# Layer norms of a two-block network on one core: statistics by column groups of the array, and a product of low rank in place of mean and shift

## The chip, the core and the metric

The kernel runs on one core of a Trainium2 chip. Its engines are TensorE (PE; its weight loads are listed as PEld), VectorE (DVE), ScalarE (ACT), GpSimd (POOL) and SyncE (SP), which issues most transfers. The metric is the device time of one execution in microseconds; less is better.

## The reference

Two blocks follow each other, in float32, on 512 tokens of 1024 features. The first has a gated delta net and a dilated attention, each with a SwiGLU feed-forward. The second is of concern here: two layers on the latents x (512 tokens, stream s=0) and on a context (256 tokens, s=1). Each layer is as follows, with ALPHA = sqrt(2) and D = 1024:

```
def layer_norm(x):
    mu = jnp.mean(xf, -1, keepdims=True)
    var = jnp.mean(jnp.square(xf - mu), -1, keepdims=True)
    return ((xf - mu) * lax.rsqrt(var + LN_EPS)).astype(x.dtype)

def modulate(x, shift, scale):
    return layer_norm(x) * (1 + scale) + shift
...
    h, hc = modulate(x, sh1, sc1), modulate(ctx, sh1x, sc1x)
    y, yc = mixing_sublayer(h, hc, ...)
    x = layer_norm(ALPHA * x + g1 * y) * ln1_g[l] + ln1_b[l]
    x = layer_norm(ALPHA * x + g2 * swiglu(modulate(x, sh2, sc2), w_ffn_in[l], w_ffn_out[l])) * ln2_g[l] + ln2_b[l]
```

The context goes the same way, but is dropped after the mixing of the second layer. So a norm is often followed at once by a second one with a modulation: normalise, scale and shift, normalise again, modulate.

## The kernel before

Everything lies transposed: a tile is 128 features (partitions) by 512 tokens of the latents or 256 of the context, and there are eight tiles, k = 0 to 7, to 1024 features. The sums of a norm go over partitions and over tiles, so TensorE makes them. Each engine has its own instruction stream, written out by hand in functions whose names begin with the engine (pe_, dve_, act_, pool_); `at(...)` and `done(...)` name semaphore values, so the order on an engine is the order of the calls.

A weight product is split: activations and weights have a high part (fp32r) and a low part, and each tile is three matmuls (high by high, low by high, high by low). `pe_products` does the mixing's products (lines L484 to L486), `pe_ffn_in` the FFN's gate and up products (L720 to L722), `pe_ffn_out` its down products (L743 to L745). The FFN works in eleven chunks; beside chunk c of the gate and up products stand the down products of chunk c-1. The products that come first after a norm are called the head here: for each tile k three pieces of the mixing (nine matmuls), or twelve matmuls of the FFN, so that they can begin when tile 0 is there.

There are five norms of the latents and three of the context in the second block: N_IN (before a mixing; in layer 1 with the end of layer 0's second norm ahead of it), N_POST (after a mixing) and N_END. The steps of one:

- `pe_stat(N, s, k)`, when tile k of the sum and its square are there. The activations are the weights of the array, 128x128 a time, and the moving side has two to four columns, ones or products of the gain (L915, and L922 for the squares); L919 adds constants. These stand between the products of the last chunk that make the tiles.
- `dve_rows` and `act_rows`: means, variances and inverse deviations, tokens on partitions, in columns of 4 or 2.
- `pe_spread`: spreads a column over all partitions, 128 tokens a matmul (L1010), and `act_spread` copies one of two to SBUF.
- for each tile, `dve_scale` (times the inverse deviation, from PSUM, L1038), `pool_centre` (less mean, L1047), `act_affine` (scale and shift); for a double norm once more; then `act_norm_part` makes the high part and `dve_norm_part` the low part (L1067), which the product of the tile waits for.

`pe_read`, the splits of weights (L566 and L665 on VectorE, L389 on ScalarE, a helper's line for all its work) and the gating of the FFN (GpSimd's casts, `pool ... R<-U`) go on beside this. The kernel sets PSUM banks by a rotating list; `PS.keep` holds one until `PS.release`.

Of the kernel before, what the change touches and what calls it, by code (L numbers as in the profile page):

```python
# [27 lines left out]
K_ID, K_ONE, K_BONE, K_EPS, K_SEL, K_RES = 0, 128, 256, 384, 389, 392  # L28
# [9 lines left out]
def constants():  # L38
# [9 lines left out]
    for s in range(2):  # L48
        k[s::32, K_SEL + s] = 1
    g = K_GDN  # L50
# [216 lines left out]
class Norm:  # L267
# [3 lines left out]
    def __init__(self, tag, streams, ready, first, to=None, second=None, key=None, h=None, hi=None, lo=None):  # L271
        self.tag, self.streams, self.ready, self.first, self.to = tag, streams, ready, first, to
        self.second, self.key, self.h, self.hi, self.lo = second, key, h, hi, lo


def build(nc, a, out):
    ctx = ExitStack()
    with ctx:
# [32 lines left out]
        by_vector = KC[:, K_SEL:K_SEL + 2]  # L311
        e1, e64, ea2, one1, e128 = (KC[:, K_EPS + n:K_EPS + n + 1] for n in range(5))
# [178 lines left out]
        def pe_products(pieces, wh, lead=1, between={}):  # L491
# [6 lines left out]
            for what, p, n, s in steps(pieces, lead):  # L498
# [21 lines left out]
                for g in group:  # L520
                    if s == (last if early else g.ends_on()):
                        pe_read(g)
                if (s, p.n) in between and early:
                    between[s, p.n]()
# [166 lines left out]
        def pe_ffn(tag, ns, then=None, mid={}, between={}, last=None):  # L691
            for c in range(12):
                if c in mid:
                    mid[c]()
                if c < 11:
                    pe_ffn_in(tag, ns, c, between)
                if c:
                    pe_ffn_out(tag, ns, c - 1, then, last)

        def pe_ffn_in(tag, ns, c, between):  # L700
# [6 lines left out]
            for i, group in enumerate(groups):  # L707
                if c == 0 and i in between:
                    between[i]()
                for j, s, p in group:  # L710
                    bank("ffn", tag, c, j, s, p)
                    pe.wait_ge(*at("wi lo", tag, c, p))
                for k in range(8):
                    for j, s, p in group:
# [8 lines left out]
                        if k == 7:  # L723
                            t.then_inc(*pe.done("product", "ffn", tag, c, j, s, p))
            pe.mark("gate up", tag, c)
            if c == 0 and "end" in between:
                between["end"]()
# [61 lines left out]
        def act_ffn(tag, ns, then=None, early=None, mid={}, taken=()):  # L789

            for c in range(12):
# [8 lines left out]
                if c < 10:  # L800
                    act_ffn_w_in(tag, c + 1)
                if c < 11:
# [10 lines left out]
        def dve_ffn(tag, ns, take_out, then=None, early=None, mid={}, taken=(), last=None):  # L813
            for c in range(12):
# [12 lines left out]
                if c == 10:  # L827
                    dve_ffn_w_out(tag, c)
                if c == 11 and early:
# [39 lines left out]
        def dve_ffn1(tag, before, l, then=None, early=None, mid={}, last=None):  # L869
# [12 lines left out]
        WZ = view(U[:, NB:NB + 48], (8, 6))  # L882
        AGB = U[:, NB + 48:NB + 64]
        CS = U[:, NB + 64:NB + 72]
        ROW = [view(U[:, NB + 72:NB + 168], (24, 4)), view(U[:, NB + 168:NB + 216], (24, 2))]
        (R_S, R_SG, R_SGG, R_SGB, R_Q, R_QGG, R_M, R_MM, R_V, R_R, R_MR, R_A, R_E, R_F, R_M2, R_W, R_V2, R_R2, R_MR2,
         R_T, R_R2A) = range(21)

        def pool_norm_weights(N, o):

            g, b = COL[:, o:o + 8], COL[:, o + 8:o + 16]
            pool.e.memset(WZ[:, :, 0], 1.0).then_inc(*pool.done("norm weights", N.tag, 0))
            pool.e.tensor_copy(WZ[:, :, 1], g).then_inc(*pool.done("norm weights", N.tag, 1))
            pool.e.tensor_tensor(WZ[:, :, 2], g, g, M).then_inc(*pool.done("norm weights", N.tag, 2))
# [2435 lines left out]
```

## Time and profile before

| | |
|---|---|
| three runs | 3733.38, 3730.15, 3723.03 us; median 3730.15 |
| the profiled execution | 3729.26 us, of it the span 3727.5 us |
| TensorE busy | 3461.7 us, 93% |
| VectorE, ScalarE, GpSimd busy | 1593.8, 1215.1, 283.6 us |
| granted TensorE clock, mean | 0.945 of full |

The profile is of one execution. The fp32 matmuls on this chip show as two records each in it, the fp32r ones as one. Lines such as L915 are those of the kernel's file. A granted clock of 1.00 is the 2.4 GHz level, 0.50 the 1.2 GHz level; a number between them is a stretch with both.

### The profile page before, as it was taken

What the parts mean: (1) busy time and instruction counts of PE and PEld (TensorE: products, weight loads), DVE (VectorE), ACT (ScalarE), POOL (GpSimd) and SP (SyncE); (2) the same over time, 40 slices, a digit from 0 to 9 for tenths busy, and PEclk for the clock granted to TensorE, in tenths of its full rate; (3) what the DMA queues carried; (4) which work ended last, traced back from release to release, by engine and by line L of the source; (5) the groups of instructions that cost most, each with busy time, mean ns of one, the idle gap of its engine ahead of it and who ended that gap; (6) DMA issues with size and microseconds to landing.
All of it is one profiled execution on the core that took longest, in us unless ns stands there. A gap on an engine that the chain in (4) does not pass through costs nothing.

```text
span 3727.5 us, 42969 instructions
## 1 busy us (share of the span) xinstructions
PE 3461.7 (93%) x18282; PEld 2891.3 (78%) x18282; DVE 1593.8 (43%) x2811; ACT 1215.1 (33%) x2006; POOL 283.6 (8%) x368
## 2 busy tenths in 40 slices
PE   7798989999999889999979978999999889889998
PEld 5685967887778768888766777888888777678887
DVE  4645544444323444344225545334443425543443
ACT  6547232212434322123224535111111425441112
POOL 1101000000000000011000003000000301020001
PEclk9899999999999899999988989999997899989998
DMA  3101021132226223131125211111110112011310
GB/s 128 41 23 68 1 91 68 68 136 79 71 90 241 71 86 113 68 113 55 46 74 200 91 46 68 68 68 68 68 44 20 38 46 94 1 68 68 136 68 34
DMA packets 190543, 282.00 MB, mean 76 GB/s; under 512 B 18952, under 2 KB 121864, under 8 KB 190224
## 3 DMA queue, kind: packets, MB, share of 16 engines
q1 hardware_dynamic: 188176, 272.19, 20.7%
q10 hardware_dynamic: 2176, 7.08, 0.6%
q8 instruction: 143, 2.34, 0.3%
q14 instruction: 48, 0.39, 0.0%
HBM read 274.00 MB, written 2.10 MB: 74 GB/s over the span
## 4 chain that ended last, share of the span: by engine, by line
PE 85%; ACT 6%; DVE 5%; POOL 2%; issue 1%; DMA 1%; SPq 1%; ACTq 0%; POOLq 0%; DVEq 0%
PE ps L720 9%; PE ps L721 9%; PE ps L722 9%; PE ps L743 5%; PE ps L484 5%; PE ps L745 5%; PE ps L744 5%; PE ps L485 5%; PE ps L486 5%; PE ps L380 3%; PE ps L374 3%; PE ps L1129 3%; ACT U L389 2%; PE ps L546 2%; PE ps L547 2%; PE ps L548 2%
## 5 line engine op out<-in xcount | busy, mean ns | idle before, releaser
L389 ACT ACTIVATE R<-ring 128x1024 fp32r<-128x1024 f32 (+4 forms) x285 | 396.6, 1415 | 1068.5 <-PE ps L722 539.6
L720 PE MATMUL ps<-R,R 128*128 128x512 f32 (+1 forms) x1760 | 657.6, 374 | 43.9 <-DVE R L665 21.2
L721 PE MATMUL ps<-R,R 128*128 128x512 f32 (+1 forms) x1760 | 654.7, 372 | 0.0
L722 PE MATMUL ps<-R,R 128*128 128x512 f32 (+1 forms) x1760 | 654.1, 372 | 0.0
L484 PE MATMUL ps<-R,R 128*128 128x512 f32 (+1 forms) x1016 | 421.8, 415 | 60.7 <-DVE ringlo L566 26.3
L720 PEld LDWEIGHTS ps<-R,R 128*128 128x128 f32 x1760 | 336.7, 191 | 106.1 <-DVE R L665 22.9
L485 PE MATMUL ps<-R,R 128*128 128x512 f32 (+1 forms) x1016 | 392.5, 386 | 0.0
L486 PE MATMUL ps<-R,ringlo 128*128 128x512 f32 (+1 forms) x1016 | 391.0, 385 | 0.0
L722 PEld LDWEIGHTS ps<-R,R 128*128 128x128 f32 x1760 | 336.0, 191 | 56.9
L721 PEld LDWEIGHTS ps<-R,R 128*128 128x128 f32 x1760 | 336.7, 191 | 56.0
L665 DVE TENSOR_TENSOR R<-ring,R 128x2048 fp32r<-128x2048 f32 x88 | 197.9, 2288 | 355.4 <-ACT R L389 355.4
L566 DVE TENSOR_TENSOR ringlo<-ring,R 128x1024 fp32r<-128x1024 f32 (+3 forms) x153 | 175.2, 1155 | 384.5 <-ACT R L389 384.5
L743 PE MATMUL ps<-R,R 128*128 128x512 f32 (+1 forms) x880 | 334.3, 380 | 3.1 <-DVE U L945 3.1
L745 PE MATMUL ps<-R,R 128*128 128x512 f32 (+1 forms) x880 | 329.5, 374 | 0.0
L744 PE MATMUL ps<-R,R 128*128 128x512 f32 (+1 forms) x880 | 329.5, 374 | 0.0
L389 ACT ACTIVATE U<-ps 128x512 f32<-128x512 f32 (+3 forms) x324 | 174.1, 553 | 440.5 <-PE ps L380 284.8
L484 PEld LDWEIGHTS ps<-R,R 128*128 128x128 f32 x1016 | 201.3, 198 | 119.3 <-DVE ringlo L566 25.9
L774 DVE TENSOR_TENSOR U<-SQ,ps 128x512 f32<-128x512 f32 (+1 forms) x110 | 69.5, 632 | 465.8 <-PE ps L722 302.5
L485 PEld LDWEIGHTS ps<-R,R 128*128 128x128 f32 x1016 | 201.5, 198 | 45.6 <-issue 12.7
L486 PEld LDWEIGHTS ps<-R,ringlo 128*128 128x128 f32 x1016 | 200.6, 197 | 37.9
L380 PE MATMUL ps<-KC,U 128*128 128x128 f32 (+2 forms) x1028 | 159.8, 295 | 50.6 <-DVE U L1853 15.6
L389 ACT ACTIVATE SQ<-ps 128x512 f32<-128x512 f32 (+1 forms) x147 | 80.5, 547 | 379.0 <-PE ps L722 375.0
(238 smaller groups left out, 4944.2 us busy)
## 6 DMA issues: line engine op xcount, KB each, us to landing
ring<-in_w_mod SPq DMA_DIRECT2D x24, 2048.0 KB, 9.4
ring<-in_ffn_w_in SPq DMA_DIRECT2D x44, 1024.0 KB, 10.9
ring<-in_w_ffn_in SPq DMA_DIRECT2D x44, 1024.0 KB, 11.3
ring<-in_ffn_w_out SPq DMA_DIRECT2D x10, 2048.0 KB, 7.7
ring<-in_w_ffn_out SPq DMA_DIRECT2D x10, 2048.0 KB, 7.8
ring<-in_dil_w_in SPq DMA_DIRECT2D x9, 2048.0 KB, 7.7
ring<-in_gdn_w_in SPq DMA_DIRECT2D x8, 2048.0 KB, 8.7
ring<-in_w_o SPq DMA_DIRECT2D x6, 2048.0 KB, 8.2
```

The costliest lines, as they stand in the source:

```text
L380: x = pe.e.transpose(o, i, ident[0:k, 0:k])
L389: return act.e.activation(o, i, fn, **kw)
L484: pe.e.matmul(ps[:, 0:x.n], hi[:, k, :], x.hi[k], start=(k == 0), stop=False)
L485: pe.e.matmul(ps[:, 0:x.n], hi[:, k, :], x.lo[k], start=False, stop=False)
L486: return pe.e.matmul(ps[:, 0:x.n], lo[:, k, :], x.hi[k], start=False, stop=(k == p.kt - 1))
L665: dve.e.tensor_tensor(WI[p][1], ffn_in_half(tag, c, p, ring), WI[p][0], SUB).then_inc(*dve.done("wi lo", tag, c, p))
L720: pe.e.matmul(ps, w[0], x[0], start=(k == 0), stop=False)
L721: pe.e.matmul(ps, w[0], x[1], start=False, stop=False)
L722: t = pe.e.matmul(ps, w[1], x[0], start=False, stop=(k == 7))
L743: pe.e.matmul(ps[:, 0:n], w[0], x[0], start=(k == 0), stop=False)
L744: pe.e.matmul(ps[:, 0:n], w[0], x[1], start=False, stop=False)
L745: t = pe.e.matmul(ps[:, 0:n], w[1], x[0], start=False, stop=(k == 1))
```

## The change

The norm is computed in another form. With r the inverse deviation and m the mean of a token, gain a and shift b of a feature, LN(x)*a + b is x*a*r plus a sum of a few products of a column (over features) by a row (over tokens): J = 2 terms for a single norm, 4 for a double one, whose two stages become one.

- **Statistics.** `pe_stat(N, P, s, p)` takes a pair of tiles p. The weights are 32 columns wide (`P.wz`), the activations and their squares move, 512 or 256 columns, and the four matmuls go to four column groups of the array (`tile_position=(0, 32 * g)`). `act_sums` copies the result to SBUF and `pe_sums` adds the groups with small matmuls of six columns, which also turns tokens onto partitions.
- **Weights of the norm.** `pool_norm_weights` (some 30 tiny operations), `dve_norm_weights`, `pe_norm_columns` (transposes), `act_norm_columns` and `dve_norm_consts` make columns and constants ahead of time, in a place `P` of SBUF. In FFN2 of layer 0 GpSimd's wait for the gate and up products of chunk 10 and stand ahead of the last chunk's casts.
- **Spread and rows.** `pe_spread` spreads one column and transposes the rows' high and low parts. `pe_rank(N, P, s, k)` is one fp32r product of 3J = 12 or 6 rows by 512 or 256 columns.
- **Tile.** `dve_scale` (x times gain column times spread row), `dve_add` (plus the rank product from PSUM), then high and low part as before. GpSimd's centring and ScalarE's affine operations are gone from here.
- **Residual.** What the double norm keeps for the residual, ALPHA*y, is made later: `pe_residual`, `act_residual`, `pool_residual` (two GpSimd operations a tile), `act_y`. In FFN2 it runs in chunk 1, in the second mixing layer behind the head.
- **Heads.** `pe_products` goes over the head's pieces tile by tile for both streams now, and calls `between[s](k)` after tile k; `pe_ffn_in` calls "tile" likewise. These issue the rank product of tile k+2.

```diff
                 early = lead > 1 and p in head
-                group = [p] if not early or s != last else head if p is head[-1] else []
+                group = [p] if not early else head if p is head[-1] else []
                 for g in group:
                     bank(*product_name(g, g.n, s))
+                    if early:
+                        PS.keep(*product_name(g, g.n, s))
                     pe.wait_ge(*at("w lo", g.tag, g.n))
                 for k in range(p.kt):
                     for g in group:
                         t = pe_tile(g, s, PS.of(*product_name(g, g.n, s)), k)
                         if k == p.kt - 1:
                             t.then_inc(*pe.done(*product_name(g, g.n, s)))
+                    if early and group and s in between:
+                        between[s](k)
...
+                    if c == 0 and s == 0 and "tile" in between:
+                        between["tile"](k)
...
-        def pe_stat(N, s, k, square=None):
...
-            for b in range(n // 128):
-                pe.e.matmul(ps[:, 8 * b:8 * b + w1.shape[1]], XS[s][:, k, b * 128:(b + 1) * 128], w1,
-                            start=(k == 0 and b == 0), stop=False)
-            if consts:
-                for j in range(8):
-                    pe.e.matmul(ps[:, 32:37], ones, WZ[:, j, 1:6], start=False, stop=False)
-            pe.wait_ge(*at("square", N.tag, s, k))
-            for b in range(n // 128):
-                t = pe.e.matmul(ps[:, 8 * b + 4:8 * b + 6], q[:, b * 128:(b + 1) * 128], w2, start=False,
-                                stop=(last and b == n // 128 - 1))
...
+            for k in (2 * p, 2 * p + 1):
+                pe.wait_ge(*at(*N.ready(s, k)))
+                pe.wait_ge(*at("square", N.tag, s, k))
+            for g, k in enumerate((2 * p, 2 * p + 1) * 2):
+                q = SQ.of(N.tag, s, k) if square is None else square[:, k, :]
+                t = pe.e.matmul(ps[32 * g:32 * g + 32, 0:n], P.wz[:, k, :], XS[s][:, k, :] if g < 2 else q[:, 0:n],
+                                start=(p == 0), stop=(p == 3), tile_position=(0, 32 * g))
+                if g > 1:
+                    t.then_inc(*pe.done("sq read", N.tag, s, k))
...
+            activate(rr[:, 0:n], PS.of("stat", N.tag, s)[:, 0:n], ACT.Copy).then_inc(*act.done("ps", "stat", N.tag, s))
...
+                t = pe.e.matmul(ps[:, 8 * b:8 * b + 6], RR.of("sums", N.tag, s)[:, b * 128:(b + 1) * 128], by_sum,
+                                start=True, stop=True)
...
+        def pe_spread(N, s):
+
+            n, J = NS2[s], N.J
+            ps = bank("spread", N.tag, s)
+            PS.keep("spread", N.tag, s)
+            pe.wait_ge(*at("rows", N.tag, s))
+            spread(ps, s, R_R if N.gain is None else R_RR, ("spread", N.tag, s))
+            ps = bank("rows", N.tag, s)
+            pe.wait_ge(*at("row parts", N.tag, s))
+            tp([(ps[0:3 * J, b * 128:(b + 1) * 128], RWF[s][:, b, 0:3 * J]) for b in range(n // 128)]).then_inc(
+                *pe.done("rows turned", N.tag, s))
...
+            pe.e.matmul(ps[:, 0:n], P.ct[s][0:3 * J, k * 128:(k + 1) * 128], P.rt[s][0:3 * J, 0:n], start=True,
+                        stop=True).then_inc(*pe.done("rank", N.tag, s, k))
...
+            dve.e.scalar_tensor_tensor(norm_to(N, s)[:, k, :], XS[s][:, k, :], AK[s][:, k:k + 1],
+                                       PS.of("spread", N.tag, s)[:, 0:NS2[s]], M, M).then_inc(
...
+            dve.wait_ge(*at("rank", N.tag, s, k))
+            dve.e.tensor_tensor(h, h, PS.of("rank", N.tag, s, k)[:, 0:NS2[s]], A_).then_inc(
...
+        def dve_tile(N, s, i):
+
+            if i < 8:
+                dve_scale(N, s, i)
+                dve_add(N, s, i)
+            if N.hi and i:
+                dve_norm_part(N, s, i - 1)
...
+            pool.e.tensor_tensor(x, x, r, M).then_inc(*pool.done("y scaled", N.tag, s, k))
...
+            pool.e.tensor_tensor(x, x, mr, SUB).then_inc(*pool.done("y centred", N.tag, s, k))
...
-            dve.e.tensor_tensor(dst[:, k, :], src[:, k, :], spread_of(N, s, part)[0], M).then_inc(
...
-            pool.e.tensor_tensor(dst[:, k, :], dst[:, k, :], RR.of("spread", N.tag, s, part)[:, 0:NS2[s]], SUB).then_inc(
...
-            activate(dst[:, k, :], dst[:, k, :], ACT.Identity, scale=g(s, k), bias=b(s, k)).then_inc(
...
+            def tile(k):
+                if k < 6:
+                    pe_rank(N, P_O, 0, k + 2)
+                if k == 7:
+                    PS.release("spread", N.tag, 0)
+                    pe_residual(N, 0)
...
-            act_ffn(tag, ns, taken=[(0, 1), (1, 1)])
+
+            def y():
+                for k in range(8):
+                    act_y(N, 0, k)
+
+            def columns_():
+                act_norm_columns(N_IN[1] if l == 0 else N_END, P_FFN)
+            act_ffn(tag, ns, mid={1: lambda: act_residual(N, 0), **({8: columns_} if l else {11: columns_})},
+                    taken=[(0, 1), (1, 1)], inner={1: y})
```

The orders of instructions show three places. The names in them: R tiles hold high and low parts, U and X activations, KC constants, ps PSUM.

TensorE in the last chunk of layer 0's first FFN of the second block, down products of the latents, before:

```order
L743 MATMUL ps<-R_1024_66,R_2048_60 128x512
L744 MATMUL ps<-R_1024_67,R_2048_60 128x512
L745 MATMUL ps<-R_1024_66,R_2048_61 128x512
L743 MATMUL ps<-R_1024_66,R_2048_60 128x512
L744 MATMUL ps<-R_1024_67,R_2048_60 128x512
L745 MATMUL ps<-R_1024_66,R_2048_61 128x512
L915 MATMUL ps<-U,X 128x4 x4
L922 MATMUL ps<-U,SQ 128x2 [waits act_result]
L922 MATMUL ps<-U,SQ 128x2 x3
L1010 MATMUL ps<-KC,U 128x128 [waits dve_result]
L1010 MATMUL ps<-KC,U 128x128 x3
```

and after:

```order
L767 MATMUL ps<-R_1024_66,R_2048_60 128x512
L768 MATMUL ps<-R_1024_67,R_2048_60 128x512
L769 MATMUL ps<-R_1024_66,R_2048_61 128x512
L1028 MATMUL ps<-X,U 32x512 [waits dve_result,act_result]
L1028 MATMUL ps<-X,U 32x512
L1028 MATMUL ps<-SQ,U 32x512 x2
L1130 MATMUL ps<-KC,U 128x128 [waits dve_result]
L1130 MATMUL ps<-KC,U 128x128
L393 MATMUL ps<-KC,U 12x128 [waits dve_result]
L393 MATMUL ps<-KC,U 12x128
```

Behind two products of one tile stood eight narrow matmuls for the statistics of one tile; now four wide ones for a pair of tiles stand behind the products. The context's spread stays where it was (L1010, now L1130) and two transposes (L393) follow it.

TensorE in the head of FFN2, layer 0, where tile 0 ends and tile 1 begins, before:

```order
L722 MATMUL ps<-R_4096_56,R_2048_61 128x512
L720 MATMUL ps<-R_4096_56,R_2048_62 128x512
L721 MATMUL ps<-R_4096_57,R_2048_62 128x512
L722 MATMUL ps<-R_4096_56,R_2048_63 128x512
L720 MATMUL ps<-R_4096_56,R_2048_60 128x512 [waits dve_result]
L721 MATMUL ps<-R_4096_57,R_2048_60 128x512
L722 MATMUL ps<-R_4096_56,R_2048_61 128x512
```

and after:

```order
L741 MATMUL ps<-R_4096_56,R_2048_62 128x512
L742 MATMUL ps<-R_4096_57,R_2048_62 128x512
L743 MATMUL ps<-R_4096_56,R_2048_63 128x512
L1160 MATMUL ps<-R_512_72,R_1024_69 128x512 [waits dve_result]
L741 MATMUL ps<-R_4096_56,R_2048_60 128x512 [waits dve_result]
L742 MATMUL ps<-R_4096_57,R_2048_60 128x512
L743 MATMUL ps<-R_4096_56,R_2048_61 128x512
```

A rank product (L1160), that of tile 2, has come in between the twelve matmuls of tile 0 and those of tile 1, which wait for VectorE in both.

VectorE in the head of FFN2, layer 1, one round and more, before:

```order
L1038 TENSOR_TENSOR X<-X,ps 128x512
L1038 TENSOR_TENSOR U<-X,ps 128x512 [waits act_result]
L1067 TENSOR_TENSOR R_4096_57<-U,R_4096_56 128x512 [waits act_result]
L1038 TENSOR_TENSOR X<-X,ps 128x512
L1038 TENSOR_TENSOR U<-X,ps 128x512 [waits act_result]
L1067 TENSOR_TENSOR R_4096_57<-U,R_4096_56 128x512 [waits act_result]
```

and after:

```order
L1170 SCALAR_TENSOR_TENSOR U<-X,U,ps 128x512
L1180 TENSOR_TENSOR U<-U,ps 128x512 [waits pe_result,dve_result]
L1190 TENSOR_TENSOR R_4096_57<-U,R_4096_56 128x512 [waits act_result]
L1170 SCALAR_TENSOR_TENSOR U<-X,U,ps 128x512
L1180 TENSOR_TENSOR U<-U,ps 128x512 [waits pe_result,dve_result]
L1190 TENSOR_TENSOR R_4096_57<-U,R_4096_56 128x512 [waits act_result]
```

The second L1038 (the double norm's second scale) is gone; the add L1180 waits for the rank product and stands ahead of the low part of the tile before (L1190).

## Rows read from the trace of the kernel before

**Rows 1.** The page, parts 1 and 4: busy time by engine; the chain that ended last.
```profile
PE 3461.7 (93%) x18282; PEld 2891.3 (78%) x18282; DVE 1593.8 (43%) x2811; ACT 1215.1 (33%) x2006; POOL 283.6 (8%) x368
...
PE 85%; ACT 6%; DVE 5%; POOL 2%; issue 1%; DMA 1%; SPq 1%; ACTq 0%; POOLq 0%; DVEq 0%
```

**Rows 2.** Windows over the span, PE alone, of L915, L922, L919, L1010 in turn.
```profile
0.00:3727.50 3727.50, 63.41 (x416) 0.95 0.22 76
...
0.00:3727.50 3727.50, 68.78 (x416) 0.95 0.22 76
...
0.00:3727.50 3727.50, 5.78 (x48) 0.95 0.22 76
...
0.00:3727.50 3727.50, 29.46 (x168) 0.95 0.22 76
```

**Rows 3.** Windows: length, busy us (instructions) by engine, PEclk, DMA share, GB/s.
```profile
2831.00:2857.00 26.00, 26.00 (x127) 24.84 (x125) 7.18 (x11) 5.70 (x11) 0.00 (x0) 0.56 0.00 1
2857.00:2907.00 50.00, 46.87 (x184) 43.30 (x184) 12.87 (x42) 12.87 (x25) 5.14 (x7) 0.50 0.00 1
3080.00:3090.00 10.00, 5.69 (x37) 4.50 (x35) 0.85 (x3) 2.05 (x4) 3.42 (x3) 1.00 0.46 157
3706.00:3728.00 22.00, 4.42 (x19) 4.03 (x19) 5.88 (x14) 8.88 (x12) 9.83 (x8) 0.50 0.25 95
```

**Rows 4.** Timeline of PE, first product of a mixing head, then of its next piece; likewise FFN.
```profile
1736.96 0.50 PE L484 MATMUL ps<-R,R 128*128 128x512 f32 x1 [2.27 <-DVE R L1067]
...
1756.12 0.77 PE L484 MATMUL ps<-R,R 128*128 128x512 f32 x1 [2.56 <-DVE ringlo L566]
...
2295.42 0.77 PE L720 MATMUL ps<-R,R 128*128 128x512 f32 x1 [5.63 <-ACT SQ L389]
...
2326.95 0.79 PE L720 MATMUL ps<-R,R 128*128 128x512 f32 x1 [5.28 <-DVE R L665]
```

**Rows 5.** Timeline of PE: start, us, operation, count; a product in four column groups.
```profile
1156.89 1.92 PE L1251 MATMUL ps<-ring,SCT 128*32 128x512 f32 x16 [0.69 <-ACT U L389]
1158.74 0.49 PE L1985 MATMUL ps<-U 64*128 64x128 f32 x4
```

**Rows 6.** Groups by shape, PE: transposes of 128 columns.
```profile
L380 PE MATMUL ps<-KC,U 128*128 128x128 f32 x992 | 154.5, 297 | 42.4 <-DVE U L1853 15.6 <-DVE U L2818 12.7 <-ACT U L389 7.5
```

**Rows 7.** Timeline of PE: products at either level of the clock, and spreads.
```profile
2299.59 0.39 PE L720 MATMUL ps<-R,R 128*128 128x512 f32 x1
2299.82 0.40 PE L721 MATMUL ps<-R,R 128*128 128x512 f32 x1
...
2868.30 0.63 PE L743 MATMUL ps<-R,R 128*128 128x512 f32 x1
2868.73 0.63 PE L744 MATMUL ps<-R,R 128*128 128x512 f32 x1
...
2921.42 1.95 PE L1010 MATMUL ps<-KC,U 128*128 128x128 f32 x16
```

**Rows 8.** Groups by shape, VectorE and GpSimd: count, busy us, mean ns, idle before.
```profile
L3080 DVE SCALAR_TENSOR_TENSOR X<-ps,MOD,X 128x512 f32<-128x512 f32 x176 | 119.6, 744 | 34.2 <-PE ps L745 34.1
...
L1067 DVE TENSOR_TENSOR R<-U,R 128x512 fp32r<-128x512 f32 x32 | 37.0, 1156 | 26.7 <-ACT R L389 26.7
...
L1038 DVE TENSOR_TENSOR U<-X,ps 128x512 f32<-128x512 f32 x32 | 21.6, 679 | 9.2 <-ACT X L389 7.8 <-PE ps L1010 1.3
...
L1047 POOL TENSOR_TENSOR X<-X,RR 128x512 f32<-128x512 f32 x32 | 40.6, 1283 | 133.7 <-ACT RR L389 119.4 <-DVE X L1038 14.3
```

**Rows 9.** Timeline of DVE, the low part in a mixing and in an FFN head.
```profile
1742.51 0.70 DVE L1067 TENSOR_TENSOR R<-U,R 128x512 fp32r<-128x512 f32 x1 [0.40 <-ACT R L389]
...
2308.48 1.50 DVE L1067 TENSOR_TENSOR R<-U,R 128x512 fp32r<-128x512 f32 x1 [1.51 <-ACT R L389]
```

**Rows 10.** Timeline of all engines, the end of the span.
```profile
3706.67 0.18 DVE L945 COPY U<-ps 128x24 f32<-128x24 f32 x1 [5.42 <-PE ps L922]
...
3714.32 9.83 POOL L1047 TENSOR_TENSOR X<-X,RR 128x512 f32<-128x512 f32 x8 [43.23 <-ACT RR L389]
```

More of the change, by code:

```diff
@@ L49, in constants @@
         k[s::32, K_SEL + s] = 1
+    for n in range(4):
+        k[n, K_SUM + n] = k[32 + n, K_SUM + n] = 1
+    for n in (64, 96):
+        k[n, K_SUM + 4] = k[n + 2, K_SUM + 5] = 1
     g = K_GDN
@@ L696, in pe_ffn @@
                     pe_ffn_in(tag, ns, c, between)
+                if c == 11 and "last" in between:
+                    between["last"]()
                 if c:
@@ L811, in act_ffn, with dve_ffn @@
                     act_square(X[:, k, :], S, then, k)
-        def dve_ffn(tag, ns, take_out, then=None, early=None, mid={}, taken=(), last=None):
+        def dve_ffn(tag, ns, take_out, then=None, early=None, mid={}, taken=(), last=None, inner={}):
             for c in range(12):
@@ new lines, in dve_norm_weights @@
+        def dve_norm_weights(N, P):
+            J = N.J
+            if N.gain is not None:
+                dve.wait_ge(*at("norm sums", N.tag))
+                dve.e.reduce_sum(P.g5s, P.g5, AX).then_inc(*dve.done("norm sum", N.tag))
+            dve.wait_ge(*at("norm weights", N.tag))
+            for s in N.streams:
+                dve.e.tensor_tensor(P.cbr[s][:, :, 2 * J:3 * J], P.cb[s][:, :, 0:J], P.cbr[s][:, :, 0:J], SUB).then_inc(
+                    *dve.done("norm column", N.tag, s))
@@ new lines, in pe_norm_columns @@
+        def pe_norm_columns(N, P):
+            for s in N.streams:
+                for i in range(2):
+                    ps = bank("columns", N.tag, s, i)
+                    pe.wait_ge(*at("norm column", N.tag, s))
+                    tp([(ps[0:3 * N.J, k * 128:(k + 1) * 128], P.cbf[s][:, 4 * i + k, 0:3 * N.J]) for k in range(4)]
+                       ).then_inc(*pe.done("columns", N.tag, s, i))
+            if N.gain is not None:
+                ps = bank("consts", N.tag)
+                pe.wait_ge(*at("norm sum", N.tag))
+                pe.e.matmul(ps[:, 0:5], ones, P.g5s, start=True, stop=True).then_inc(*pe.done("consts", N.tag))
@@ L1043, in pool_centre, with spread @@
-        def pool_centre(N, s, k, part):
-            dst = N.h[s] if part else N.to[s] if N.to else XS[s]
-            pool.wait_ge(*at("scaled", N.tag, s, part, k))
-            pool.wait_ge(*at("spread mean", N.tag, s, part))
-            pool.e.tensor_tensor(dst[:, k, :], dst[:, k, :], RR.of("spread", N.tag, s, part)[:, 0:NS2[s]], SUB).then_inc(
-                *pool.done("centred", N.tag, s, part, k))
-            if k == 7:
-                pool.mark("rr read", "spread", N.tag, s, part)
-        def act_affine(N, s, k, part):
-            dst = N.h[s] if part else N.to[s] if N.to else XS[s]
-            g, b = (N.second if part else N.first)
-            act.wait_ge(*at("centred", N.tag, s, part, k))
-            activate(dst[:, k, :], dst[:, k, :], ACT.Identity, scale=g(s, k), bias=b(s, k)).then_inc(
-                *act.done("h" if part else "y", N.tag, s, k))
+        def spread(o, s, row, name):
+            for b in range(NS2[s] // 128):
+                t = pe.e.matmul(o[:, b * 128:(b + 1) * 128], ROW[s][:, row, b:b + 1].broadcast_to([128, 128]), ident,
+                                start=True, stop=True)
+            t.then_inc(*pe.done(*name))
@@ L2535, in pe_in, with context @@
-            pe_products(in_pieces(l), WHM[l], 3, between)
+            N, P = N_IN[l], P_FFN
+            def context(k):
+                if l and k < 6:
+                    pe_rank(N, P, 1, k + 2)
+                if l == 0 and k == 0:
+                    pe_stat(N, P, 0, 3)
+                if l == 0 and k == 1:
+                    pe_sums(N, 0)
+                if l and k == 7:
+                    PS.release("spread", N.tag, 1)
+                if k == 6 - 2 * l:
+                    pe_spread(N, 0)
+                if k == 7:
+                    pe_rank(N, P, 0, 0)
+                    pe_rank(N, P, 0, 1)
```

737 lines of the change are left out of this document (423 added, 314 removed).

## The prediction

> **What bounds the kernel now.** I read the page first: TensorE is busy for 93% of the span and makes 85% of the chain that ended last [rows 1]. So what comes off TensorE counts in full, unless TensorE then waits for another engine. Next I read the changed lines over the whole span [rows 2]: the statistics (L915, L922, L919) hold TensorE for 63.41 + 68.78 + 5.78 = 138.0 us in 880 records, the spreads (L1010) for 29.46 us in 168. A record takes 5.78/48 = 0.12 us for the constants, at the full clock, and 132.2/832 = 0.16 in the mean of the others, for two to five moving columns. Then I read the granted clock by stretch [rows 3]: from 2831 to 2907 us, where the statistics stand between down products of the second block's first FFN, it is 0.56 and then 0.50, although TensorE is busy for 46.87 of the last 50 us. Last I read the heads of the products that follow a norm [rows 4, 9]: there TensorE runs products nearly back to back, and VectorE makes the tiles just ahead of it.
>
> The sum is made against the profiled execution, 3729.26 us (span 3727.5), 0.9 us under the median of the three runs, 3730.15. A measurement of this kernel can tell about 0.3%, 11 us, from no change.
>
> **Statistics, -104.** Each pair of tiles of the latents now takes four fp32 matmuls of 512 columns in four column groups; each pair of the context four of 256. The nearest row is another fp32 product in four column groups, L1251 [rows 5]: its 16 records start at 1156.89 and the next line starts at 1158.74, 1.85 us. With two records a matmul that is eight matmuls, two rounds of four groups, if the groups run side by side; a pair is one round, 0.93 us. I take 1.0, and 0.57 for the context. There are 20 and 12 pairs: 26.8 us. The 26 small matmuls of the sums are 52 records; 16 spread records took 1.95 us [rows 7], 0.12 each: 6.3 us. With 1 us for three constant matmuls that is 34, for 138: -104. If the groups ran one after another, a pair would cost up to four times as much, 4 x 0.93 and 4 x 0.43: (3.7 - 1.0) x 20 + (1.7 - 0.57) x 12 = +68. Against it: the row's 16 records would then take 0.12 us each, while even an fp32r product of 512 columns starts its next only after 0.23 [rows 7].
>
> How the array is entered is a place where notes and rows can be weighed. The row shows nothing between L1251 and its neighbour beyond the 1.85 us, so the sum has only the rounding up from 0.93 to 1.0. The Trainium skill ("TensorEngine Tiling (Array Packing)", Key Properties) says that changing the tiling mode drains TensorE. An estimate for such a drain is what a product lasts beyond the next start, 0.39 - 0.23 = 0.16 us [rows 7]; with a change in and out of 32 groups that would be 10 us, where the sum has some 4.
>
> **Spreads, transposes, ranks, +10.** 29.5 us go. What comes: 54 fp32 spreads, 108 records of 0.12, 13 us; 90 transposes, priced by 992 of 128 columns in 154.5 us [rows 6], 0.155 each, 14 us; 40 fp32r rank products of 512 columns at 0.23 [rows 7] and 24 of 256 at half of it, 12 us.
>
> **Clock, -16.** Products of 512 columns start every 0.43 us at the half level and every 0.23 at the full one [rows 7]. From 2831 to 2907 stand 48 such at the half level, and 30 of 256 columns. As the near-empty matmuls around them go, I take them at the full level: 48 x 0.20 + 30 x 0.09 = 12, and 4 more in small stretches elsewhere. The bound on the other side is nothing, if the stretch keeps its level.
>
> **The rank loop, +47.** In a head the program issues rank k+2 on TensorE after product k, while VectorE works in the order scale i, add i (waits for rank i), low part i-1. Product k+1 waits for low part k+1; that stands behind add k+2, which waits for rank k+2, which stands behind product k. So TensorE can't run on; its order is product k, rank k+2, idle for the add and the low part, product k+1. Only the scale lies under the product. Prices: the add as L1038, 0.68 us [rows 8], the low part 0.70 where nothing disturbs it [rows 9], the rank until its end 0.39 [rows 7], some 0.05 for hand-overs. In a mixing head a step is nine matmuls, 2.05 us; a period becomes 3.85. Before, the head takes from 1736.96 to 1756.12 less the last wait of 2.56 [rows 4], 16.6 us; afterwards seven periods and a product, 29: +12. In an FFN head a step is twelve matmuls, 2.74 us; a period becomes 4.54, the head 34.5 us. Before, it takes from 2295.42 to 2326.95 less 5.28 [rows 4], 26.3 us: there the start is at the half clock and VectorE and GpSimd pace it. +8. Two heads of each kind make +40. The context's head of the second mixing layer, 256 columns, has a period of some 2.24 by the same sum, 16.8 us for about 10 now: +7. Behind the heads TensorE waits for a weight split, 5.28 us [rows 4]; VectorE gets no free time for it in the longer head, so nothing is given back. If a step's waits were all hidden the term would be nothing; a low part as slow as its mean, 1.16 [rows 8], would make it +62.
>
> Here a rule bears. The rows show the low part at 1.50 us in an FFN head, where GpSimd's L1047 runs, and at 0.70 in a mixing head [rows 9]; I let it be 0.70 afterwards, since GpSimd's work leaves the heads. The Trainium skill ("SBUF — State Buffer", Two separate sides) says that VectorE and GpSimd share a pair of ports and that the loser is blocked for the whole operation; the trace agrees.
>
> **The residual elsewhere, +12.** The 64 GpSimd operations of 1.28 us [rows 8] no longer pace the heads, but in each FFN2 sixteen of them, 20.5 us, stand ahead of chunk 1's casts, which its down products wait for, and eight affine operations stand ahead of ScalarE's silu. A chunk of these products lasts about as long as the head, 25 us or more, so most is covered; what sticks out I take as 3 us in each layer. The tiny operations of the norm's weights wait on GpSimd for the gate and up products of the last chunk and stand ahead of its casts: +3. In the second mixing layer the residual's copies and spreads stand ahead of the next weight split: +3. With the covers gone each would be some 10; fully covered, nothing.
>
> **The tail, 0.** Before, the last norm runs from 3706.67 to the end, GpSimd's eight centrings being 9.83 us of it [rows 10]. Afterwards VectorE does a scale with a column, 0.744, and an add, 0.68, per tile [rows 8], 11.4 us; no affine follows the last, but a copy, the sums' matmuls and a transpose stand ahead. These even out to within 2 us.
>
> Sum: -104 + 10 - 16 + 47 + 12 = -51, 3729.3 - 51 = **3678 us**.
>
> **The rivals.**
> (a) The loop costs nothing, because tiles are ready early. For it: the heads run nearly back to back now. Against: the order leaves no rank in stock behind the first two. Then 3678 - 47 = 3631.
> (b) The other side, slower. In the loop TensorE is busy for 2.05 of 3.85 us or 2.74 of 4.54, and the granted clock may fall to the half level in it. Twelve products then cost 12 x 0.20 = 2.4 us more and the rank 0.2: two FFN heads of eight steps +42, two mixing heads (nine products, 2.0) +32, the context's +7: +81, to 3759. It decides from 63 us of these on, some three quarters of the steps. For it: after long idle the clock was low, 0.50 from 3706 on. Against: from 3080 to 3090 TensorE was busy for only 5.69 of 10 us in short pieces, and the clock was 1.00 [rows 3].
> (c) The clock of 2831 to 2907 isn't won back and the covers of the residual fail in part: +16 and some +17: 3711.
> (d) The column groups run one after another: 3678 + 68 = 3746. The row of L1251 speaks against it.
>
> **How the numbers follow.** The forecast has 0.58, its own range 3655 to 3700 (the clock's 16 and the loop's size either way); (a) 0.13, (c) 0.14, (b) 0.11, (d) 0.04. The range from 3635 to 3738 leaves out (b), (d) and a part of (a). Faster, under 3719: the forecast, (a) and half of (c), 0.79; within 0.3%: the rest of (c) and edges of (b), 0.08; slower: most of (b) and (d), 0.13.
>
> **What would show it.** Afterwards: the statistics of a pair in some 1 us, four groups starting together; TensorE waiting for VectorE's low part in each of the eight steps of a head, 1.4 to 1.8 us each; heads longer by 8 to 12 us; the clock near 1.0 from 2800 on to the next idle; GpSimd busy in FFN2's second chunk instead of the heads; a span near 3676. Wrong if the heads show no wait in each step (a), if their matmuls start every 0.43 us (b), if the four groups start one after another (d), or if chunk 1 shows a new wait of over 5 us on casts (c).

## The result and the profile after

The change made the kernel slower: 3772.51 us median of four runs, against 3726.59 before in the same series, a ratio of 1.0127 (95% interval 1.0098 to 1.0156), 46 us. Forecast were 3678 us, in 3635 to 3738.

The page of the changed kernel, parts 1 and 4:

```profile
span 3772.1 us, 42206 instructions
## 1 busy us (share of the span) xinstructions
PE 3444.7 (91%) x17810; PEld 2808.0 (74%) x17810; DVE 1609.8 (43%) x2884; ACT 1175.3 (31%) x1960; POOL 263.5 (7%) x410
...
PE 84%; DVE 6%; ACT 6%; issue 1%; DMA 1%; POOL 1%; ACTq 0%; SPq 0%; DVEq 0%; POOLq 0%
```

TensorE is busy for 17 us less, not for over 100 less [rows 1], and the span is longer by 44.6 us. The rest of the span is idle time of TensorE: 327 us now, 266 before.

What the statistics cost on TensorE is as forecast. Here is a pair of tiles of the latents on TensorE's timeline with the products beside it (two lines each for the activations and the squares, two records a line):

```profile
2278.07 0.39 PE L499 MATMUL ps<-R,ringlo 128*128 128x512 f32 x1
2278.39 0.62 PE L1028 MATMUL ps<-X,U 128*32 128x512 f32 x2
2278.41 0.62 PE L1028 MATMUL ps<-SQ,U 128*32 128x512 f32 x2
2278.85 0.60 PE L1028 MATMUL ps<-X,U 128*32 128x512 f32 x2
2278.86 0.60 PE L1028 MATMUL ps<-SQ,U 128*32 128x512 f32 x2
2279.39 0.50 PE L497 MATMUL ps<-R,R 128*128 128x512 f32 x1
```

All four column groups start within 0.02 us; from 2278.39 to the next product at 2279.39 it is 1.00 us, as I had taken, and 0.09 more ahead of it, since a further product would have followed the L499 of 2278.07 after 0.23. The groups by shape of the new lines (the two lines of L1028 lie over each other, so their 22.8 us are one and the same time):

```profile
L1028 PE MATMUL ps<-SQ,U 128*32 128x512 f32 x80 | 22.8, 650 | 0.0
...
L1028 PE MATMUL ps<-X,U 128*32 128x512 f32 x80 | 22.8, 647 | 11.8 <-ACT SQ L402 11.8
...
L1130 PE MATMUL ps<-KC,U 128*128 128x128 f32 x108 | 18.2, 324 | 18.2 <-DVE U L1114 14.4 <-DVE U L1099 3.1 <-DVE U L1170 0.7
...
L1160 PE MATMUL ps<-R,R 12*128 12x512 f32 x24 | 12.5, 541 | 0.7 <-ACT R L402 0.7
...
L1049 PE MATMUL ps<-KC,RR 128*128 128x6 f32 x52 | 7.6, 267 | 5.5 <-ACT RR L402 5.5
```

TensorE's waits, with total, times and longest:

```profile
PE ps L497 <- DVE R L1190: 25.4, 18, 2.7
...
PE ps L741 <- DVE R L1190: 20.0, 13, 2.6
...
PE ps L1130 <- DVE U L1114: 14.4, 4, 4.9
...
PE ps L1028 <- ACT SQ L402: 13.4, 8, 4.8
...
PE ps L1049 <- ACT RR L402: 5.5, 5, 3.0
```

The wait for the low part (L1190) is 45.4 us in 31 places; before it was 14.8 us for L1067 in 11. The waits of L1028 and L1049 are new, and the spreads (L1130) wait 18.2 us for rows, as the row of their group says, against 11.3 before.

The first mixing head on TensorE, three of its steps:

```profile
1743.03 0.51 PE L497 MATMUL ps<-R,R 128*128 128x512 f32 x1 [1.45 <-DVE R L1190]
...
1747.24 0.50 PE L497 MATMUL ps<-R,R 128*128 128x512 f32 x1 [1.45 <-DVE R L1190]
...
1750.47 0.79 PE L1160 MATMUL ps<-R,R 6*128 6x512 f32 x1
1752.72 0.79 PE L497 MATMUL ps<-R,R 128*128 128x512 f32 x1 [1.45 <-DVE R L1190]
1753.31 0.63 PE L498 MATMUL ps<-R,R 128*128 128x512 f32 x1
1753.73 0.63 PE L499 MATMUL ps<-R,ringlo 128*128 128x512 f32 x1
...
1756.85 0.79 PE L1160 MATMUL ps<-R,R 6*128 6x512 f32 x1
1759.49 0.80 PE L497 MATMUL ps<-R,R 128*128 128x512 f32 x1 [1.85 <-DVE R L1190]
```

From 1743.03 to 1747.24 a step takes 4.21 us: the nine products at the full clock, the rank product, 1.45 us idle. From 1752.72 to 1759.49 it takes 6.77 us, and the products (L498 at 1753.31, L499 at 1753.73) start every 0.42 us. VectorE in the step that ends at 1747.24:

```profile
1742.89 0.74 DVE L1170 SCALAR_TENSOR_TENSOR U<-X,U,ps 128x512 f32<-128x512 f32 x1
1745.90 0.69 DVE L1180 TENSOR_TENSOR U<-U,ps 128x512 f32<-128x512 f32 x1 [2.27 <-PE ps L1160]
1746.50 0.68 DVE L1190 TENSOR_TENSOR R<-U,R 128x512 fp32r<-128x512 f32 x1
```

The scale is done early; the add waits 2.27 us for the rank product, and the low part stands behind it. That is the loop that the prediction drew. The windows tell what it had not drawn in: the first mixing head, the first FFN head, the two stretches of [rows 3], and one in an attention.

```profile
1725.00:1767.00 42.00, 32.16 (x78) 21.15 (x78) 12.92 (x20) 4.32 (x8) 4.94 (x8) 0.64 0.10 33
2307.00:2353.00 46.00, 37.08 (x111) 26.58 (x112) 14.52 (x23) 6.28 (x9) 1.01 (x2) 0.76 0.00 0
2831.00:2857.00 26.00, 26.00 (x142) 22.64 (x141) 8.06 (x13) 2.90 (x3) 7.66 (x32) 1.00 0.19 61
2857.00:2907.00 50.00, 38.35 (x238) 26.38 (x236) 25.62 (x69) 16.82 (x33) 0.00 (x0) 0.88 0.00 1
2038.00:2076.00 38.00, 38.00 (x139) 24.66 (x137) 15.05 (x50) 16.53 (x54) 0.00 (x0) 0.51 0.18 63
```

The granted clock is 0.64 and 0.76 in the heads. From 2831 to 2857 it is 1.00, where it had been 0.56 [rows 3], and from 2857 to 2907 it is 0.88 in place of 0.50.

Where the 44.6 us of the two spans lie I read by laying the n-th matmul of a product's line in one trace beside the n-th in the other (columns: stretch in the trace before, how much later the changed kernel is at its end than at its beginning):

| stretch before, us | change, us |
|---|---|
| up to 1480 | +3.0 |
| statistics and rows of the norms: 1480 to 1737, 2191 to 2295, 2791 to 2916, 3250 to 3321, 3638 to the end | -81 |
| head of the first mixing, 1737 to 1756 | +24.6 |
| FFN head of layer 0, 2295 to 2327 | +19.7 |
| both heads of the second mixing, 2916 to 2961 | +37.8 |
| FFN head of layer 1, 3321 to 3352 | +20.3 |
| an attention, 2040 to 2057 | +11.3 |
| all else | +9 |

### The profile page after: what moved, and what is told of

Its sections match the earlier page's. It is cut to its first block, busy times and chain, and to the rows that moved or that the text cites. A ratio compares the mean times of both kernels' runs of the same rounds, so it can differ in the third digit from the quotient of the medians.

```text
span 3772.1 us, 42206 instructions
## 1 busy us (share of the span) xinstructions
PE 3444.7 (91%) x17810; PEld 2808.0 (74%) x17810; DVE 1609.8 (43%) x2884; ACT 1175.3 (31%) x1960; POOL 263.5 (7%) x410
## 4 chain that ended last, share of the span: by engine, by line
PE 84%; DVE 6%; ACT 6%; issue 1%; DMA 1%; POOL 1%; ACTq 0%; SPq 0%; DVEq 0%; POOLq 0%
PE ps L741 10%; PE ps L742 10%; PE ps L743 10%; PE ps L497 6%; PE ps L498 5%; PE ps L499 5%; PE ps L767 4%; PE ps L769 4%; PE ps L768 4%; PE ps L393 4%; PE ps L387 3%; PE ps L1277 3%; PE ps L563 2%; PE ps L564 2%; PE ps L565 2%; PE ps L413 2%
## 5 line engine op out<-in xcount | busy, mean ns | idle before, releaser
L741 PEld LDWEIGHTS ps<-R,R 128*128 128x128 f32 x1760 | 339.2, 193 | 119.7 <-DVE R L1190 28.6
L498 PE MATMUL ps<-R,R 128*128 128x512 f32 (+1 forms) x1016 | 399.9, 394 | 0.0
L499 PE MATMUL ps<-R,ringlo 128*128 128x512 f32 (+1 forms) x1016 | 398.9, 393 | 0.0
L743 PEld LDWEIGHTS ps<-R,R 128*128 128x128 f32 x1760 | 339.1, 193 | 58.5
L742 PEld LDWEIGHTS ps<-R,R 128*128 128x128 f32 x1760 | 339.2, 193 | 56.9
L497 PEld LDWEIGHTS ps<-R,R 128*128 128x128 f32 x1016 | 206.0, 203 | 152.2 <-DVE R L1190 32.4
L498 PEld LDWEIGHTS ps<-R,R 128*128 128x128 f32 x1016 | 206.5, 203 | 45.9 <-issue 12.2
L499 PEld LDWEIGHTS ps<-R,ringlo 128*128 128x128 f32 x1016 | 205.6, 202 | 39.6
L393 PE MATMUL ps<-KC,U 128*128 128x128 f32 (+5 forms) x1118 | 174.4, 297 | 49.4 <-DVE U L2001 16.0
```

The source lines that it names most:

```text
L393: x = pe.e.transpose(o, i, ident[0:k, 0:k])
L497: pe.e.matmul(ps[:, 0:x.n], hi[:, k, :], x.hi[k], start=(k == 0), stop=False)
L498: pe.e.matmul(ps[:, 0:x.n], hi[:, k, :], x.lo[k], start=False, stop=False)
L499: return pe.e.matmul(ps[:, 0:x.n], lo[:, k, :], x.hi[k], start=False, stop=(k == p.kt - 1))
L741: pe.e.matmul(ps, w[0], x[0], start=(k == 0), stop=False)
L742: pe.e.matmul(ps, w[0], x[1], start=False, stop=False)
```

## The experiments

The theory after the result (A) was: the loop makes TensorE idle in every step as forecast, and this idle time lets the granted clock fall in the heads, which the forecast's sum had left out. Its rivals: VectorE has too much work per tile (B), or the low clock has another cause (C). The ratios below are each to the kernel before in the run's own series.

**The low part first.** In `dve_tile`, which all heads use:

```diff
             if i < 8:
                 dve_scale(N, s, i)
-                dve_add(N, s, i)
             if N.hi and i:
                 dve_norm_part(N, s, i - 1)
+            if i < 8:
+                dve_add(N, s, i)
```

> Edit: in dve_tile the low part of tile i-1 stands ahead of the add of tile i, so that product k+1 no longer waits for rank k+2. In the trace of the changed kernel the four heads of the latents and the context's head are 103 us longer than before, of which TensorE waits 45 us for the low part (L1190) and the rest is products starting every 0.43 us. Theory A (the loop, and the clock that falls because of its waits): both go; a mixing step becomes 9 products and a rank, 2.28 us, an FFN step 2.97, and the run 3665 to 3680. Theory B (VectorE's three operations per tile are too much work, 2.13 us, whatever their order): the order changes little, less than 20 us gained, 3750 or more. Theory C (waits go, the clock stays low for another reason): 3715 to 3730.

Measured: 3685.59 us, ratio to before 0.9899 (0.9877 to 0.9920). That is 87 us less than the changed kernel, for three lines in another order. Part 1 of its page, and TensorE's waits in it:

```profile
PE 3395.7 (92%) x17810; PEld 2775.9 (75%) x17810; DVE 1611.5 (44%) x2884; ACT 1176.1 (32%) x1960; POOL 265.1 (7%) x410
```

```profile
PE ps L1130 <- DVE U L1114: 14.5, 4, 4.9
...
PE ps L1028 <- ACT SQ L402: 13.4, 8, 4.8
...
PE ps L497 <- DVE R L1190: 3.9, 3, 2.1
...
PE ps L741 <- DVE R L1190: 2.0, 1, 2.0
```

45.4 us have become 5.9, and the waits around the statistics stayed. Its first mixing head and first FFN head:

```profile
1722.00:1745.00 23.00, 22.12 (x78) 14.95 (x78) 13.80 (x20) 4.61 (x8) 5.79 (x8) 0.93 0.15 49
2278.50:2307.60 29.10, 29.07 (x118) 21.50 (x118) 15.97 (x24) 6.20 (x8) 1.02 (x2) 0.95 0.00 1
```

The clock is 0.93 and 0.95, and TensorE is busy for 22.12 of 23 us. VectorE now runs ahead:

```profile
1726.36 0.69 DVE L1180 TENSOR_TENSOR U<-U,ps 128x512 f32<-128x512 f32 x1 [2.52 <-PE ps L1160]
1726.97 0.74 DVE L1170 SCALAR_TENSOR_TENSOR U<-X,U,ps 128x512 f32<-128x512 f32 x1
1727.75 0.69 DVE L1190 TENSOR_TENSOR R<-U,R 128x512 fp32r<-128x512 f32 x1
1729.05 0.69 DVE L1180 TENSOR_TENSOR U<-U,ps 128x512 f32<-128x512 f32 x1 [0.61 <-PE ps L1160]
```

It still waits for rank products, but with a step in hand. B has fallen: the operations are the same. The time is 5 us over the upper end of my expectation. Laid beside the trace before as in the table above, its five heads are still 23.5 us longer, so some 79 of their 102 us came back; I had expected nearly all.

**The rank product a step earlier.** VectorE's order as in the changed kernel:

```diff
-                if k < 6:
-                    pe_rank(N, P, 0, k + 2)
+                if k < 5:
+                    pe_rank(N, P, 0, k + 3)
...
                     pe_rank(N, P, 0, 1)
+                    pe_rank(N, P, 0, 2)
```

The same in the context's head and in the FFN's.

> Edit: VectorE's order as in the changed kernel, but three rank products stand ahead of the head and rank k+3 is issued after product k. This cuts the same loop at its other place. Theory A: the same as with the low part first, 3665 to 3680. Theory B: 3750 or more. If only one of the two cuts helps, the loop as I drew it is not the whole of it.

Measured: 3689.25 us, ratio 0.9912 (0.9893 to 0.9932). That is 9 us over the 3680 at the end of my range. But the other place where the loop can be cut gives the same within the intervals, so the loop is as drawn.

**Both.**

> Edit: both cuts together. Theory A: no more than either alone, 3665 to 3680, since one slack of a product is enough; up to 5 us less where a rank's latency still shows.

Measured: 3683.20 us, ratio 0.9899 (0.9875 to 0.9923): no more than one cut, as expected, and again a little over the range.

**The loop kept, the idle time filled.** Behind each rank k+2 in the heads stand five more products that nothing reads:

```diff
+        def pe_fill(N, s, k):
+            ps = bank("fill", N.tag, s, k)
+            for i in range(5):
+                t = pe.e.matmul(ps[:, 0:NS2[s]], N.hi[s][:, k, 0:128], N.hi[s][:, k, 0:NS2[s]], start=True, stop=True)
+            t.then_inc(*pe.done("ps", "fill", N.tag, s, k))
```

> Edit: the loop stays, but five more fp32r products of 512 columns (256 for the context), of which nothing is used, follow each rank k+2 in the heads, 1.15 us in the 1.45 us that TensorE idles there. Theory A: the clock in the heads stays near 1.00, the heads take 29 and 34.5 us as forecast for the loop alone, and the run becomes 45 to 60 us faster for more work: 3712 to 3728. If the low clock isn't due to the idle time: nothing gained, 3770 or a few more, and products still every 0.43 us in part of each head.

Measured: 3725.98 us, ratio to before 1.0010 (0.9988 to 1.0031), 46.5 us less than the changed kernel for more work. A step of its first mixing head, and the windows of that head and the FFN's:

```profile
1742.84 0.50 PE L497 MATMUL ps<-R,R 128*128 128x512 f32 x1
...
1745.10 0.50 PE L1160 MATMUL ps<-R,R 6*128 6x512 f32 x1
1745.53 1.42 PE L1166 MATMUL ps<-R 128*128 128x512 f32 x5
1747.05 0.50 PE L497 MATMUL ps<-R,R 128*128 128x512 f32 x1
```

```profile
1727.50:1760.00 32.50, 31.85 (x108) 21.21 (x108) 12.45 (x19) 3.84 (x7) 5.81 (x8) 0.89 0.13 42
2295.00:2333.00 38.00, 37.39 (x147) 26.31 (x145) 15.04 (x23) 6.19 (x8) 0.61 (x1) 0.95 0.00 0
```

From 1742.84 to 1747.05 the step takes 4.21 us, just what it takes in the changed kernel where the clock is full. The fill (L1166) costs the step nothing; what it changes is the clock: 0.89 and 0.95 for 0.64 and 0.76. C has fallen, and the two costs of the loop stand apart: 46.5 us are the clock, 3725.98 - 3685.59 = 40 us the idle time. The ten times of this run go from 3710.83 to 3741.69 us, and by the ratios the two costs are 44 and 41 us, so each is known to some 10 us. The pages and traces say the same: from the changed kernel to the one with the low part first, TensorE's busy time falls by 3444.7 - 3395.7 = 49 us for the same instructions and its idle time by 327.4 - 287.7 = 40 us. The five heads are 40.6 us shorter with the fill than without, and another 38 with the low part first.

**The statistics alone.** On the kernel before, its `pe_stat` is replaced by the wide form with weights of ones:

```diff
-            for b in range(n // 128):
-                pe.e.matmul(ps[:, 8 * b:8 * b + w1.shape[1]], XS[s][:, k, b * 128:(b + 1) * 128], w1,
...
+            for g in range(4):
+                j = k - 1 + g % 2
+                t = pe.e.matmul(ps[32 * g:32 * g + 32, 0:n], ones[:, 0:32], XS[s][:, j, :] if g < 2 else PAIR[g % 2][:, 0:n],
+                                start=(k == 1), stop=last, tile_position=(0, 32 * g))
```

> Edit of the kernel before, the statistics alone: per pair of tiles four fp32 matmuls of 32 columns of ones by 512 or 256 columns in four column groups, in place of the narrow ones and of the 24 of the constants. Spreads, tiles and heads are as before. What it leaves out: the sums that the rows then read aren't the norm's (the variance is held at 1 or more), so the output isn't the reference's. My terms: 32 pairs at 27 us for 138, -111, and the clock from 2831 to 2907 at full level, -16, would give about 3596 for a median of 3722. What the runs so far suggest (theory A2): the last pair of each norm now waits for its squares and the rows for TensorE's few products, some 15 to 20 us of new waits, so 3610 to 3630. Rival: if the narrow matmuls were not what held the clock low, it stays near 0.50 there and the run comes out 12 to 16 us longer than that, 3625 to 3645.

Measured: 3640.06 us, ratio 0.9779 (0.9740 to 0.9817), 82 us less than before by the ratio, where my terms said 127 and the theory's correction 92 to 112. Both were too high, and by its time alone the run falls into the range that I had given the rival, 3625 to 3645; the granted clock has to decide. A first and a second stretch of the last chunk of the first FFN, with its rows and statistics:

```profile
2785.00:2802.00 17.00, 14.28 (x117) 11.37 (x115) 9.09 (x16) 5.53 (x11) 0.00 (x0) 1.00 0.00 1
2802.00:2835.00 33.00, 17.46 (x85) 10.42 (x86) 18.49 (x65) 15.88 (x33) 7.95 (x11) 0.76 0.00 1
```

The clock is 1.00 in the first stretch, where wide statistics stand between the products; before, it was 0.56 there, with TensorE busy throughout. So the low clock of [rows 3] went with the narrow matmuls, and the rival has fallen. But from 2802 on TensorE is busy for only 17.46 of 33 us: it waits above all for the rows, which narrow statistics no longer cover, and the clock is 0.76.

**The statistics twice.** On the kernel with the low part first:

```diff
+                for again in range(2):
                     t = pe.e.matmul(ps[32 * g:32 * g + 32, 0:n], ..., tile_position=(0, 32 * g))
```

> Edit of the kernel with the low part first: every statistics matmul is issued twice in a row (the sums are doubled, so the output isn't the reference's). It measures the price of the new statistics by itself: 27 us if a pair costs 1.0 and 0.57 as I took it, 31 us with the 1.14 and 0.62 that the changed kernel's trace shows, so 3713 to 3719 against 3685.6; 4 x that if the groups ran one after another (over 3780).

Measured: 3711.40 us, ratio 0.9945 (0.9924 to 0.9965), 26 us over the 3685.59, and by the two ratios 17 us. Its ten times are from 3689.19 to 3715.17, with a gap between 3697 and 3709, so the price is known to about 10 us only. It excludes groups one after another.

**The wait for the context's rows.** On the kernel with the low part first, in layer 0's output product:

```diff
-                             2: lambda: ranks(0), 3: third, 4: lambda: pe_residual(N, 1)})
+                             3: lambda: ranks(0), 4: third, 5: lambda: pe_residual(N, 1)})
```

and so for the spread and on ScalarE and VectorE.

> Edit of the kernel with the low part first: in layer 0's output product the context's spread, ranks and tiles stand one piece later on all engines. TensorE waits there 4.92 us for the rows. If this wait is the exposed chain of rows, the run gains 3 to 5 us (3681 to 3683); if the wait only moves to the piece behind, nothing.

Measured: 3690.53 us, ratio 0.9897 (0.9868 to 0.9925), the same as without the edit. In its trace the spreads wait 9.6 us for rows (L1114) in place of 14.5, but the statistics wait 17.5 us for squares in place of 13.4: the wait has moved. A gain of 3 us could still hide in the interval.

**The new statistics, whole, with the old tile.** On the kernel before, also the copy, the sums and the gain's columns, and nothing of the rest of the change:

```diff
+                w = WIDE[N.tag][:, j, :] if N.second else ones[:, 0:32]
...
+            activate(SUMS(N)[:, 0:n], PS.of("stat", N.tag, s)[:, 0:n], ACT.Copy)
...
+                t = pe.e.matmul(ps[:, 8 * b:8 * b + 6], SUMS(N)[:, b * 128:(b + 1) * 128], by_sum,
```

> Edit of the kernel before: only the statistics in the new form, now whole: four column groups a pair, the copy, the small matmuls of the sums, the constants as before; spreads, centring on GpSimd, affine on ScalarE and the residual stay as before. It computes the reference. The statistics alone, without copy and sums, gave 3640 for 3728 before. The sums add 52 records of 0.12, 6 us, and eight copies, of which three stand in the open at 1 us each: 3645 to 3655. If this holds, the new tile (rank product, scale and add on VectorE, residual later) loses 35 to 45 us against the old one even with the low part first (3685.6). The rival, that the new tile is neutral and the garbled sums made the earlier run fast, gives 3680 or more.

Measured: 3654.09 us, ratio 0.9818 (0.9795 to 0.9842), 71 us less than before (3724.97 in this series). It beats both kernels and the repaired change. Part 1 of its page:

```profile
PE 3355.5 (92%) x17758; PEld 2762.9 (76%) x17758; DVE 1593.2 (44%) x2811; ACT 1217.1 (33%) x2014; POOL 285.8 (8%) x383
```

TensorE is busy for 106 us less than before [rows 1] and idle for 292 us in place of 266: 26 us of what the new statistics save are lost in new waits.

The rest of the change without its loop costs 3685.59 - 3654.09 = 31 us more than the old tile. Not all of this is the tile. In the two profiled executions, 36 us apart, 17.6 us lie in the stretch with layer 0's attention, 1857 to 2171 of the trace before, whose instructions are the same in all three kernels: against before it is 11.6 us shorter with the new statistics and 6.0 longer with the low part first, and the half level of the clock holds for 40, 71 and 80 us of it (new statistics, before, low part first). The heads make 19 us, and the residual some 14; in the stretches of the statistics the kernel with the low part first is 12 us ahead.

## Why the prediction was wrong, step by step

Two steps of the prediction failed, each by nearly 50 us: the clock in the heads, which the sum left at the full level, and the gain of the new statistics, which it took without any new wait.

The medians make a chain from the kernel before to the changed one: new statistics -71, the rest of the change without the loop +31, the loop's idle time +40, the clock in the loop +46.5. That these sum to +47, for 46 measured, proves nothing, as each link begins where the last ends. Forecast were -120 (statistics and their clock), +22, +47 and 0: off by +49, +9, -7 and +46.5.

- **Statistics, -104, and clock, -16.** The prices held: 1.00 us a pair, with 0.09 ahead of it, and four groups side by side; the clock from 2831 to 2857 is full, though 0.88 behind that. What failed is the silent step beside them, that no wait takes their place. Alone they brought -82, where these terms without the sums were -127; with the sums they brought -71 for -120. The narrow matmuls had been 138 us of work on the path, but also the cover under which squares and rows were made. Now TensorE waits 13.4 us for squares, above all of a norm's last pair, 5.5 us for the copied sums and 7 us more than before at the spreads; it had waited some 8 us at such places. With the new statistics whole and the old tile, idle time rose by 26 us, and in its trace the stretches of statistics and rows are 67 us shorter. The rest of the 49 that are missing no run takes apart.
- **Spreads, transposes, ranks, +10, and the residual, +12.** Together with the tile they measure +31 against the old tile. In the trace, chunk 1 of the two FFN2 holds 1.9 and 3.8 us of it, for 3 each forecast. In the second mixing layer I had 3 us, for the copies and spreads; but the eight operations of `act_y` stand there ahead of ScalarE's next work, and the first matmul of the attention waits for them in every kernel with the new tile:

```profile
3114.00 5.73 ACT L402 ACTIVATE X<-X,U 128x512 f32<-128x512 f32 x8
...
3119.88 2.50 PE L1277 MATMUL ps<-U 64*128 64x256 f32 x10 [6.41 <-ACT X L402]
```

These 6.4 us are in neither the kernel before nor the one with the new statistics alone. How the rest divides over 90 transposes, 64 rank products and rows is not shown, and up to 18 of the 31 us can be the attention's clock.

- **The rank loop, +47.** Right in its mechanism, 40 measured. A step is 4.21 us at the full clock for my 3.85: the rank starts 0.1 us after the products, and result, add and low part take 1.45 us idle behind a rank of 0.50. The low part took 0.68 or 0.69 us in all but one of the latents' 32, as I had let it; but my reading of [rows 9] was incomplete. GpSimd's L1047 ran in the mixing head before as well, 8.49 us for five from 1737.59, so 1.70 each where the mean is 1.28; there it was mostly GpSimd that was slowed, and in the FFN head mostly VectorE.
- **The clock in the loop.** This is rival (b), to which I gave 0.11. I priced all products of the heads at the full clock, on one window of 10 us, 3080 to 3090, with TensorE at 5.69 of 10 us and the clock at 1.00 [rows 3]. I called that short pieces, and it is not: TensorE ran nearly without a break until 3086.5, and then stood idle for 5.44 us, across the window's end. The rows behind, of the same trace, show that the clock fell:

```profile
3090.00:3097.00 7.00, 5.10 (x22) 3.95 (x23) 6.14 (x23) 6.75 (x18) 4.00 (x3) 0.51 0.01 2
```

```profile
3091.90 1.97 PE L380 MATMUL ps<-KC,U 128*128 128x128 f32 x8 [5.44 <-ACT U L389]
```

So this row was no evidence against (b). The head's own windows have 0.64 and 0.76, and 46.5 us are about six tenths of rival (b)'s 81. (b) alone, from 3678, would have come to 3759, near the 3772.51 measured, but by luck in part: its clock was too dear by 35 us, and the statistics' gain, which it took from the forecast, too large by 49.

- **Rival (a)**, 3631 without any loop: the cut loop gives 3685.59, and 37 us under its own series' before where (a) had 98. So even without the loop the statistics and the tile were short by some 60 us.
- **Tail, 0.** It held: from the first rows to the end 20.8 us before [rows 10]; from the copied sums, 3749.99, to 3772.1 it is 22.1.

The Trainium skill's drain at a change of tiling mode ("TensorEngine Tiling (Array Packing)", Key Properties) is small here: a pair took 1.09 us with the gap ahead of it, and half of the row in [rows 5] is 0.93. If that row holds no change itself, this leaves 0.16 for both changes, half of the 0.32 of my estimate: 5 us for 32 pairs, not 10.

Open: the attention of the second block from 2038 to 2076, 37.5 us long, ran at 0.50 in the changed kernel with no idle time in it. The same stretch had 13.7 us of the half level before, and 27 in the kernel with the low part first, whose attention the change does not touch either. It made 11 of the 44.6 us between the two profiled executions. Whether it comes from where in time the idle stretches ahead of it fall was not tried, and neither was how far it differs between executions of one kernel.

## What to carry to other kernels

When an operation of a second engine is made to wait for a matmul that stands behind the current product, follow the ring through both instruction orders; here two engines waited for each other in nearly every step of five heads, and exchanging two calls was worth 87 us. A repeated wait cost twice here, 40 us as idle time and 46.5 as clock: give the products next to such waits a price at either level of the clock, and look at the rows behind an idle stretch, not only at those in it. Look also at the clock of stretches that an edit does not touch before its whole difference is put down to it. And before work is taken off the critical engine, ask which chain runs under it: 138 us of narrow matmuls went for some 37 of wide ones and sums, and 71 us came out.

## What the runs showed of the hardware

- Five useless products in each idle stretch of 1.45 us raised the granted clock of the first mixing head from 0.64 to 0.89 and left the step at 4.21 us; the run became 46.5 us faster.
- With fp32 matmuls of two to four moving columns between its products, TensorE was busy for 26.00 of 26 us at a clock of 0.56 and for 46.87 of 50 us at 0.50 [rows 3]; with wide statistics in their place these stretches had 1.00 and, with new idle time, 0.88.
- After 5.44 us without a matmul, until 3091.90 in the trace before, the clock was 0.51 from 3090 to 3097.
- Four column groups of 128x32 weights with 512 moving fp32 columns start within 0.02 us of each other and take 1.00 us for eight records.
